# The second mixer's attention between the k-tiles of its projections, and a norm on VectorE

## The reference

```
# first model, layer 1 (x comes from a gated delta-rule mixer, layer 0)
kv   = rms_norm(x, kv_norm_g) @ w_kv             # keys, values: 8 heads of 128 each
proj = rms_norm(x, b_norm_g) @ b_w_in            # queries (8 x 128) and gate z (1024)
s    = q k^T * 128**-0.5 + rel_bias[bucket(i-j)], causal   # one block of 256 keys
o    = softmax(s) v
x    = x + (o * silu(z)) @ b_w_out
x    = rms_norm(x, final_norm_g)                 # the first model's output
# second model, layer 0: even mixer
h    = rms_norm_2(x, l0_attn_norm)
proj = h @ l0_w_in                               # latents 416 wide, then q, k, v of "stick breaking"
...                                              # MLA attention and stick-breaking attention, 8 heads each
x    = x + concat(mla, sb) @ l0_w_o
x    = x + swiglu(rms_norm_2(x, ...))            # width 2816
# second model, layer 1: "fox" attention (16 heads of 64, a decay per head), then swiglu
```

## Time and profile before

| what | value |
|---|---|
| median of 3 runs | 1029.9 us |
| the profiled execution | 1029.2 us, span 1027.0 us |
| TensorE matmul busy | 973.2 us, 95% of the span |
| VectorE, ScalarE, GpSimd busy | 654.5, 482.8, 45.1 us |
| DMA queue of the weights | 145.61 MB, 44.1% of 16 engines' span |
| granted TensorE clock, whole span | 0.985 |

### The profile page before, as it was taken

How to read it: one execution, slowest core, us unless ns; L and a number is a source line. 1 busy time by engine, 2 the same in 40 slices (tenths; PEclk the granted TensorE clock), 3 DMA queues, 4 the chain that set the end, 5 groups by cost and what they waited for, 6 DMA issues and landing times.

```text
span 1027.0 us, 16185 instructions
## 1 busy us (share of the span) xinstructions
PE 973.2 (95%) x6364; PEld 865.9 (84%) x6364; DVE 654.5 (64%) x1111; ACT 482.8 (47%) x822; POOL 45.1 (4%) x45
## 2 busy tenths in 40 slices
PE   5999899998997797989999999999999999999998
PEld 5999799887896686866899999888766689999886
DVE  5786975766356478857666565546767566565643
ACT  5469321363446362755643433445556563333431
POOL 2002000000000004300000000001000000000000
PEclk9999899999999898999999999999999999999999
DMA  9434330245554043612365655555433145555550
GB/s 333 137 124 139 98 124 2 102 164 205 164 168 145 1 144 113 198 49 83 124 195 173 188 180 183 186 186 167 146 119 120 46 144 183 185 182 179 189 184 20
DMA packets 106280, 148.27 MB, mean 144 GB/s; under 512 B 12548, under 2 KB 59328, under 8 KB 106096
## 3 DMA queue, kind: packets, MB, share of 16 engines
q1 hardware_dynamic: 104318, 145.61, 44.1%
q0 software_dynamic: 704, 1.77, 0.5%
q10 hardware_dynamic: 1202, 0.13, 0.1%
HBM read 146.03 MB, written 1.45 MB: 144 GB/s over the span
## 4 chain that ended last, share of the span: by engine, by line
PE 84%; DVE 9%; ACT 4%; issue 1%; DMA 1%; SPq 0%; DVEq 0%; ACTq 0%
PE ps L1802 23%; PE ps L1803 22%; PE ps L1804 22%; PE ps L1892 3%; DVE wlo L1114 2%; ACT whi L644 1%; PE ps L2008 1%; PE ps L2400 1%; DVE G L1260 1%; PE ps L2373 1%; PE ps L2018 1%; PE ps L2013 1%; PE ps L1928 1%; DMA raw<-in_a_w_in 1%; PE ps L2399 1%
## 5 line engine op out<-in xcount | busy, mean ns | idle before, releaser
L1114 DVE TENSOR_TENSOR wlo<-raw,whi 128x1024 fp32r<-128x1024 f32 (+1 forms) x272 | 323.7, 1231 | 168.8 <-ACT whi L644 168.6
L644 ACT ACTIVATE whi<-raw 128x1024 fp32r<-128x1024 f32 (+1 forms) x272 | 271.3, 1047 | 334.7 <-PE ps L1804 332.2
L1802 PE MATMUL ps<-xh,whi 128*128 128x256 f32 x1088 | 312.4, 287 | 3.8 <-DVE wlo L1114 3.8
L1803 PE MATMUL ps<-xl,whi 128*128 128x256 f32 x1088 | 309.3, 284 | 0.0
L1804 PE MATMUL ps<-xh,wlo 128*128 128x256 f32 x1088 | 309.1, 284 | 0.0
L1802 PEld LDWEIGHTS ps<-xh,whi 128*128 128x128 f32 x1088 | 210.4, 193 | 5.2 <-DVE wlo L1114 3.0
L1803 PEld LDWEIGHTS ps<-xl,whi 128*128 128x128 f32 x1088 | 210.5, 193 | 0.1
L1804 PEld LDWEIGHTS ps<-xh,wlo 128*128 128x128 f32 x1088 | 210.2, 193 | 0.0
L1802 PE MATMUL ps<-whi,xh 128*128 128x512 f32 (+1 forms) x192 | 80.2, 418 | 5.3 <-DVE wlo L1114 5.0
L1804 PE MATMUL ps<-whi,xl 128*128 128x512 f32 (+1 forms) x192 | 75.4, 393 | 0.0
L1803 PE MATMUL ps<-wlo,xh 128*128 128x512 f32 (+1 forms) x192 | 75.3, 392 | 0.0
(11 more groups left out here) (384 smaller groups left out, 1291.8 us busy)
## 6 DMA issues: line engine op xcount, KB each, us to landing
raw<-in_l_w_gate SPq DMA_DIRECT2D x44, 512.0 KB, 3.9
raw<-in_l_w_up SPq DMA_DIRECT2D x44, 512.0 KB, 4.9
raw<-in_l_w_down SPq DMA_DIRECT2D x44, 512.0 KB, 4.6
raw<-in_l_w_in SPq DMA_DIRECT2D x36, 512.0 KB, 4.2
raw<-in_a_w_in SPq DMA_DIRECT2D x32, 512.0 KB, 4.7
raw<-in_w_kv SPq DMA_DIRECT2D x16, 512.0 KB, 4.7
raw<-in_b_w_in SPq DMA_DIRECT2D x16, 512.0 KB, 4.7
raw<-in_l_w_o SPq DMA_DIRECT2D x16, 512.0 KB, 4.5
```

What stands on the lines that cost most here:

```text
L644: nc.scalar.activation(whi[:, g % HIGH, a], raw[:, g % RAW, a], ACT.Copy).then_inc(hi_done, 1)
L1114: nc.vector.tensor_tensor(wlo[:, g % LOW, a], raw[:, g % RAW, a], whi[:, g % HIGH, a].bitcast(F32), ALU.subtract).then_inc(lo_done, 1)
L1802: mm(o_, a_h, b_h, start=start, stop=False, skip_group_check=True)
L1803: mm(o_, a_h, b_l, start=False, stop=False, skip_group_check=True)
```

## The change

The attention's helper by pairs goes on all three engines; in its place `second(s)` runs a head at a time in slots 0 to 39: 0 to 15 are the values' k-tiles, 16 to 31 the gate's, 32 to 39 the first eight of the output projection. The queries come ahead of the values, the bias windows between the halves of the queries' second chunk. The scores use banks 4 and 5, the transposes bank 6, the values' product bank 7. The probabilities have four buffers of one head each instead of two of a pair. The output of a head is copied to b_qT, over its own queries, and gate product, high part and low part are done four heads at a time. The output projection goes by rows. `spread("nc")` moves from slot 3 to slot 4, and one split of the MLA stage is emitted a little earlier. The normalisation of x moves from GpSimd to slot 36 of VectorE's program of the MLA stage, as one instruction for each token tile. `gfin` has its own memory for that.

```diff
+        B_S, B_T, B_V = (1, 3, 5, 7, 9, 11, 13, 15), (4, 6, 8, 10, 12, 14, 16, 18), (9, 10, 11, 12, 17, 18, 19, 20)
+        Z_AT = (24, 32)
-        LAT_T, KV_AT, Q_AT = 5, 7, 11
+        SPREAD_AT, LAT_T, KV_AT, Q_AT = 4, 5, 7, 11
         U_BK = base(chunks("w_kv", 0, 2))
+        U_BQ = base(chunks("b_w_in", 0, 2))
         U_BV = base(chunks("w_kv", 2, 2))
-        U_BQ = base(chunks("b_w_in", 0, 2))
         U_BZ = base(chunks("b_w_in", 2, 2))
-        U_BO = base(chunks("b_w_out", 0, 2))
+        U_BO = base(lambda: by_rows("b_w_out"))
...
# GpSimd
-            pool.wait_ge(S("gfin_in"), 16)
-            pool.wait_ge(*past("nfin", "root", 1))
-            link(nc.gpsimd.tensor_tensor(x[:], x[:], rms["nfin"][1].unsqueeze(2).to_broadcast([P, NT, D]), ALU.mult))
-            link(nc.gpsimd.tensor_tensor(x[:], x[:], gfin[:].unsqueeze(1).to_broadcast([P, NT, D]), ALU.mult))
...
# ScalarE
+            ln_exp()
+            hi_until(U_BV + 1)
+            act.wait_ge(S("bias_ps"), 4)
...                                           # eight copies of the bias windows
+            def second(s):
+                for h in at_slot_of(B_V, s - 1):
+                    act.wait_ge(*past("b", "pv", h + 1))
+                    nc.scalar.activation(b_qT[:, h, :], ps[:, 7, T * (h % 2):T * (h % 2) + T], ACT.Copy).then_inc(step("b", "out_sb"), 1)
+                for h in at_slot_of(B_T, s - 1):
+                    act.wait_ge(*past("b", "pT", h + 1))
+                    if h >= 4:
+                        act.wait_ge(*past("b", "pv", h - 3))
+                    nc.scalar.activation(b_pT[:, h % 4], ps[:, 6, 0:3 * P], ACT.Copy).then_inc(step("b", "pTs"), 1)
+                for c in range(2):
+                    if s == 8 * c + 8:
+                        evacuate("nb", U_BV, J_BV, c, b_v[:, :, 512 * c:512 * c + 512])
+                if s % 4 == 0:
+                    hi_until(U_BV + s // 4 + 2)
+                for h in at_slot_of(B_S, s - 1):
+                    act.wait_ge(*past("b", "max", 2 * (h + 1)))
+                    for tt in range(NT):
+                        s_ = b_s[:, h % 4, SPAN[tt]]
+                        nc.scalar.activation(s_, s_, ACT.Exp, bias=b_max[:, h % 4, 0, tt:tt + 1],
+                                             accum_out=b_max[:, h % 4, 1, tt:tt + 1]).then_inc(step("b", "exp"), 1)
+                if s == 22:
+                    nc.scalar.preload_act_table(ACT.Silu)
...                                           # s == Z_AT[c]: silu, wait for the gated half, its high part
# VectorE
+            def second(s):
+                for h in at_slot_of(B_T, s):
+                    dve.wait_ge(*past("b", "exp", 2 * (h + 1)))
...                                           # reciprocal, two products
+                for h in at_slot_of(B_S, s - 1):
+                    dve.wait_ge(*past("b", "sc", h + 1))
...                                           # scale and bias, two maxima
+                    if s == Z_AT[c]:
+                        scaled_fm(U_BZ, J_BZ, c, b_zT)
+                    if s == Z_AT[c] + 1:
+                        dve.wait_ge(S("z_silu"), c + 1)
+                        nc.vector.tensor_tensor(b_qT[:, a, :], b_qT[:, a, :], b_zT[:, a, :], ALU.mult).then_inc(S("b_gated"), 1)
+                    if s == Z_AT[c] + 2:
...                                           # low part of the half
+            for s in range(B_SLOTS):
+                if s % 4 == 1:
+                    lo_until(U_BV + s // 4 + 2)
+                second(s)
...
+                if s == 36:
+                    for tt in range(NT):
+                        link(nc.vector.scalar_tensor_tensor(x[:, tt, :], x[:, tt, :], r1[:, tt:tt + 1], gfin[:], ALU.mult, ALU.mult))
...
# TensorE
+            def second(s):
+                for h in at_slot_of(B_V, s):
+                    t = slice(T * (h % 2), T * (h % 2) + T)
+                    pe.wait_ge(*past("b", "pTs", h + 1))
+                    pe.wait_ge(acc_read["A"], read_by("A", J_BV + h // 4))
+                    if h:
+                        pe.wait_ge(*past("b", "out_sb", h))
...                                           # two matmuls: 256 and 128 columns
+                for h in at_slot_of(B_T, s):
+                    pe.wait_ge(*past("b", "p", 2 * (h + 1)))
...                                           # three transposes
+                for h in at_slot_of(B_S, s):
...                                           # two matmuls: 128 and 256 columns
+            fm(U_BQ, J_BQ, xh, xl)
+            fm(U_BQ + 2, J_BQ + 1, xh, xl, between=bias_windows)
             for c in range(2):
-                tm(U_BV + 2 * c, J_BV + c, zh, zl)
+                tm(U_BV + 2 * c, J_BV + c, zh, zl, after=lambda k: second(8 * c + k))
...
+            for c in range(2):
+                fm(U_BZ + 2 * c, J_BZ + c, xh, xl, after=lambda k: second(16 + 8 * c + k))
+            tm_rows(U_BO, J_BO, zh, zl, each=lambda k: pe.wait_ge(*past("b", "out", k // 4 + 1)),
+                    after=lambda s: second(32 + s), inside=lambda: turn_x("nc", 0, x, J_BO))
```

More of the change, by code:

```diff
@@ L225, in block_kernel @@
         fox_max = small(16).rearrange("p (a w t) -> p a w t", a=4, w=2)
-        soft = {n: small(16).rearrange("p (a w t h) -> p a w t h", a=2, w=2, t=NT) for n in ("b",)}
+        b_max = small(16).rearrange("p (a w t) -> p a w t", a=4, w=2)
         def tok(n):
@@ L293, in block_kernel @@
         M_S, M_T, M_V = (23, 23, 24, 25, 26, 27, 28, 29), (25, 26, 27, 28, 29, 30, 31, 32), (26, 27, 28, 29, 30, 31, 32, 33)
-        c_at = lambda table, s: [n for n, slot in enumerate(table) if slot == s]
+        at_slot_of = lambda table, s: [n for n, slot in enumerate(table) if slot == s]
         fox_at = lambda table, s: [h for h in range(16) if table[h] == s]
@@ L710, in between @@
                 hi_until(u1 + 3)
[L712 to L730, removed]
-                                                     accum_out=mx[:, i % 2, 1, tt, n:n + 1])\
-                                    .then_inc(step(name, "exp"), 1)
-                    h = i - 3
-                    if h >= 0:
-                        src, to = pair_out(name, h)
-                        if name == "b":
-                            act.wait_ge(S("b_gated"), h + 1)
-                            src = b_t[:, h % 2, :].rearrange("p (a t) -> p a t", a=2)
-                        else:
-                            act.wait_ge(*past(name, "pv", h + 1))
-                        nc.scalar.activation(zh[:, to], src, ACT.Copy).then_inc(step(name, "out_hi"), 1)
             def ln_exp():
@@ L876, in _ @@
             hi_until(U_BK + 4)
-            for c in range(2):
-                hi_until(U_BV + 2 * c + 2)
+            hi_until(U_BQ + 2)
             for n in range(2):
@@ L893, in _ @@
-            for c in range(2):
-                hi_until(U_BZ + 2 * c + 4)
-                act.wait_ge(acc_read["D"], read_by("D", J_BZ + c))
-                nc.scalar.activation(b_zT[:, 4 * c:4 * c + 4, :], b_zT[:, 4 * c:4 * c + 4, :], ACT.Silu).then_inc(S("z_silu"), 1)
-            hi_until(U_BO + 2)
-            ln_exp()
-            softmax("b")
-            between("nc", gain_fc, xh, U_BO, 4, J_BO, U_C, squared="nfin")
+            ln_exp()
+            hi_until(U_BV + 1)
+            act.wait_ge(S("bias_ps"), 4)
@@ L901, in _ @@
+            for s in range(B_SLOTS):
+                second(s)
+            between("nc", gain_fc, xh, U_BO, 4, J_BO, U_C, squared="nfin", rows=True)
             for c in range(2):
@@ L985, in mla_out @@
             def mla_out(s):
[L987 removed]
+                for h in at_slot_of(M_V, s - 1):
                     if h % 2:
@@ L1508, in _ @@
+            for s in range(B_SLOTS):
+                if s % 4 == 1:
+                    lo_until(U_BV + s // 4 + 2)
+                second(s)
+            between("nc", gain_fc, xh, xl, added(U_BO, J_BO, rows=True), U_BO, U_C, rows=True)
             dve.wait_ge(S("gfin_in"), 16)
```

252 lines of the change are left out of this document (93 added, 159 removed).

## The result

| | before | after |
|---|---|---|
| median | 1029.7 us (4 runs) | **1005.0 us** (1004.8 to 1007.7, 4 runs) |
| ratio | | 0.977, 95% interval 0.975 to 0.979 |
| profiled execution, span | 1029.2, 1027.0 us | 1004.8, 1002.9 us |
| granted clock, whole span | 0.985 | 0.991 |

The account below looks back on a forecast made before the run. TensorE, busy 95% of the span, was taken as the bound, so only its standstills and lower-clock stretches could give time. Attention 12.6 plus norm 8.5, 21.1 us off 1029.9, gave 1008.8 us, range 1005 to 1016.

Parts of the forecast that it names:

- The attention: Second mixer's attention: dealing heads over k-tile slots replaces a 29.5 us stage by 16.9 us of slots, gaining 12.6 us.
- the price of heads between k-tiles: Values, gate and output projection slots: the heads' matmuls and switching losses, priced from the MLA stage, add 16.9 us.
- The 0.17: Interleaved slots with values: a k-tile ahead of values takes 1.57 us instead of 1.40, so 0.17 us is lost.
- best case: Second mixer's attention: heads without any switching losses cost 8 x 1.85 = 14.8 us, a gain of 14.7 us.
- The norm: Behind the output projection: without GpSimd's two products VectorE runs freely, the latents' transposes come at 394.6, gaining 8.5 us.
- Rival (b): Behind the output projection: GpSimd doesn't hold VectorE, or another GpSimd product does; the 8.5 us don't come, 1017 us; 4%.
- the idles that stayed: TensorE behind the output projection: two idles of 0.6 and 0.7 us stay, clock kept; if it falls, 2.0 us lost.
- The cover of 0.6 us at slot 36: End of MLA's output projection: residual ends at 497.0, TensorE needs it at 497.65; uncovered, up to 2.4 us lost.
- The rule: SBUF port pair: a VectorE instruction with two SBUF inputs waits for a whole GpSimd instruction that reads SBUF.
- The output projection by rows: Second mixer's output projection: the same 96 matmuls in another order, put at 0 us, at worst 1.
- Rival (a): Interleaved attention: heads wait as in the MLA stage, giving back 5 us, 1014 us; 11%.
- rival (c): Interleaved slots: TensorE falls to the lower clock; with all of them 30 us more, 1039 us; 3%.

Follow-up runs that it names:

- norm-only kernel: The kernel before with only the normalisation of x moved to VectorE's slot 36, the attention still a stage by itself: 1020.1 us, ratio 0.990.
- the later edits: Changed kernel with the next weight unit's split ahead of the root and latents' transposes a slot later (1006.6 us), or with six GpSimd memsets added (1009.4 us).
- the memsets: The changed kernel with six chained GpSimd memsets of 128x1536 at the time of the old products, the norm staying on VectorE: 1009.4 us.

## Why the prediction came out as it did

**The attention (12.6 forecast, 16.6 measured).** The mechanism held: no waits, full clock, the stage of 29.5 us replaced by its matmuls. The term that was mis-sized is the price of heads between k-tiles, 16.9 us for 13.1 by the slots. It was taken from the earlier trace rows, and those rows have tiles 64 wide; 2.5 us of the difference came back when the same widths were put into this mixer. The 0.17 that I read in the earlier trace rows as lost ahead of values is also in part (0.08) the loss behind the transposes that stand in front of that k-tile, which the sum has already. The "best case" 14.7 of the prediction wasn't even a bound, since it kept those durations.

**The norm (8.5 forecast, 8.7 measured).** The mechanism held. The links came as they were worked out: low parts at 1.2, the addition at 0.15, transposes at 394.60 in the norm-only kernel against 394.6. Rival (b) fell with the product back on GpSimd. The clock kept its level over the idles that stayed, as taken; behind waits of 1.82 and 2.77 us in the same place it didn't, in the later edits. The cover of 0.6 us at slot 36 held. The rule that I read as "GpSimd that reads SBUF against two SBUF inputs" was enough for this edit and is half of what the memsets showed.

**What was missing.** 1.2 us of clock in the MLA stage, 58 us behind the end of the output projection. I had asked only whether the clock would fall in the stretches that change, and the earlier trace rows name only those. On the other side, the shift shrinks by 1.5 us after 472. Of it 0.7 comes at 678: TensorE waits 0.5 us for a weight unit's low part, behind a small transfer (wf) that lands 3.8 us after its issue instead of 2.9 (3.7 to 3.9 and 2.9 to 3.0 over the traces). All eleven traces with the norm on VectorE have this, and none of the three with it on GpSimd, so it goes with the move and is a price that the sum lacks; why the transfer is longer stays open. The other 0.8 is the last transfer of the output, 3.6 us instead of 2.8, which comes in six of the fourteen traces. The 1.2 gained and the 1.5 lost cancel in the total: that is luck, as neither was in the sum.

**What was put at nothing.** The bias windows, the order of queries and values, the table load: no wait shows. The output projection by rows: nothing as an exchange, but a wait of 1.6 us without it. Rival (a) didn't come, and one slot less of distance brings it in full; rival (c), 20 slots at the lower clock, had no sign.

## What to carry to other kernels

Work with a latency chain between its matmuls costs only those matmuls (and what is lost in the tile behind) once it is dealt out over another product's tiles, if the slots between its steps outlast the chain: here three slots of 1.4 us and their heads did, and two cost 8 us. Take the price of a dealt-out step from rows that have the same tile in the array, not only the same columns. An instruction of two columns that took microseconds was here, each time, one that another engine held. Moving the other work to a place where nobody waits gave 8.7 us; splitting it in place gave nothing, since the hold goes both ways. And a clock drop of 1 to 1.5 us in one trace of each kernel can't be put down to the kernel: first see whether it also comes and goes where nothing was changed.

## What the runs showed of the hardware

- A 64-wide tile costs more than a 128-wide one: 0.33 us a head, 0.08 of it in the k-tile ahead and 0.10 in the product behind, with the same streamed columns. 96 rows for 128 cost nothing.
- Beside a GpSimd memset a `tensor_scalar` of 2 columns takes up to 1.44 us and a `tensor_tensor` 0.16; beside a GpSimd product the `tensor_tensor` of 2 columns takes 4.53.
- The hold between GpSimd's products and VectorE's products with two SBUF inputs goes both ways: a GpSimd product of 128x192 takes 0.50 us alone and 0.95 to 2.01 beside one of VectorE's, ending 0.36 us behind it. Eight of them took 7.67 us for one of 128x1536 in 4.27.
- The same stretch with the same 2.0 us wait ran at a granted clock of 0.83 in five kernels and 1.00 in four, 1.2 us apart; and 240 to 275, behind the same two waits and with the same 33.79 us of matmul, read 1.00 in four traces and 0.95 in ten, 1.5 us apart. What decides it stays open.
